# Value and gate columns of the recurrence as a seven-product Strassen stage per segment, x prepared elsewhere, the recurrence one lag deeper

## The chip, the cores and the metric

The kernel runs on one core of one Trainium2 chip. The metric is the device time of one execution in microseconds (us); before the change it is 2083.62 us, the median of three runs (2082.52 to 2084.76).

## The reference, cut to what matters

One decoder layer on x of 2048 tokens by 1024 features. Everything is float32.

```python
h = rms_norm(x, norm_w) * (1 + scale) + shift          # scale, shift, gate from c @ w_ada
proj = h @ w_in                                        # 1024 -> 6656 columns
aq, ak, av, ag, rq, rf, ri, rg = split(proj)           # 1024, 256, 256, 1024, 4 x 1024
attn = sliding_window_attention(rope(norm(aq)), rope(norm(ak)), av, sinks) * silu(ag)
f = lb + (1 - lb) * sigmoid(rf)
rec = hgrn2_chunkwise(rq, f, ri)                       # 8 heads, chunks of 64 tokens
rec = rms_norm(rec, rec_norm_w) * silu(rg)
out = x + gate * (concat(attn, rec) @ w_out)
```

The change concerns the columns ri (the value) and rg (the gate) of the projection: 2 x 1024 of the 6656 columns.

## The kernel before, in words

Each large product is made in split precision: an operand is rounded to a high part (ScalarE, `split_hi`, `round_x`) and the rest is subtracted (VectorE, `split_lo`, `rest_x`), and TensorE makes three products, high x high, high x low and low x high (`split_products`, L498 to L503). Every matmul of the projections and of the output is issued from L502.

The tokens are worked in two segments of 1024. A segment has two phases, and at the end of each all five queues (SP, TensorE, ScalarE, VectorE, GpSimd) meet (`arrive`, `meet`).

- Ahead of the first segment, w_ada is loaded in six parts of 2 MB, TensorE multiplies it by c, and VectorE reads out shift, scale and gate (L484 to L496, L1007 to L1069).
- Attention: four groups of four heads, eight token blocks of 128 each (`att_iter`). In group 0 of a segment the blocks of x are prepared between the iterations: square, root on GpSimd, scaling, eight transposes on TensorE (`transpose_x`, L551), modulation, rounding, rest. Three stages of the attention of earlier blocks (scores, probabilities, output) run beside the projections of the present block.
- Recurrence: eight heads, two quads of 512 tokens each (`rec_iter`, L647 to L703). For a quad TensorE makes f and q (columns by tokens: 24 matmuls of 512 columns each), then value and gate as rows (`project_nat`, L542: two halves of 48 matmuls of 256 columns), and beside them the chunk products of the quad before it: k_inv x q_dec and the transposes of k_out (L664, L667), the chunk states (L678), the two parts of the output (L694, L700). ScalarE makes tanh, the logarithm and three exponentials, VectorE the running sum, the states (L1274) and the normed rows (L1287), GpSimd three products and a root.
- The output: 16 rows of blocks, each 96 matmuls of 512 columns (`out_rows`, L742).

The order of the work on each engine is the order in which its queue is written; there is no planner. SP issues all transfers in one queue. Spills of the attention and of the recurrence go to DRAM and come back for the output (`load_mixed`).

Of the kernel before, what the change touches and what calls it, by code (L numbers as in the profile page):

```python
# [16 lines left out]
KT = D // P  # L17
SEQ = 2048
# [14 lines left out]
UNITS = GROUPS + RHEADS  # L33
# [4 lines left out]
MOD_T = 3 * D // HALF  # L38
WO_PARTS = 8
WO_F = FT // WO_PARTS  # L40
WO_EARLY = 5
# [7 lines left out]
ATT_UNIT, REC_UNIT = REG[0] + REG[1], KT * 4 * RK  # L49
LAG = 3  # L50
TWO_PI = 2.0 * np.pi
# [5 lines left out]


def hybrid_layer(nc, x, cT, pos, norm_w, w_ada, b_cols, b_gate, w_in, qk_w, sinks, rec_w, lbT, w_out,
                 ident_d, masks_d, causal_d, freq_d, out, mixed_T, mixed):  # L60
    with ExitStack() as ctx:
# [4 lines left out]


        def sbuf(where, name, shape, dt=F32):
            return where.enter_context(nc.sbuf_tensor(name, shape, dt))

        ident = sbuf(ctx, "ident", [P, P])
        gate_bc = sbuf(ctx, "gate_bc", [P, D])

        unsplit = ExitStack()
        h_f = sbuf(unsplit, "h_f", [P, KT, SEG])
        x_early = sbuf(unsplit, "x_early", [P, KT, SEG])

        ang, turns, cosv, sinv = [x_early[:, :, (NBLK - 3) * P + q * (HD // 2):(NBLK - 3) * P + (q + 1) * (HD // 2)]
                                  for q in range(4)]

        wa = [h_f[:, t * KT // 2:(t + 1) * KT // 2, :].rearrange("p k (a n) -> p (k a) n", n=HALF) for t in range(2)]
        wa += [sbuf(unsplit, f"wa{t}", [P, KT, HALF])[:] for t in (2, 3)]
        unsplit.close()
        main = ExitStack()
        h_lo = sbuf(main, "h_lo", [P, KT, SEG], F32R)
        h_hi = sbuf(main, "h_hi", [P, KT, SEG], F32R)
        w_hi = [sbuf(main, f"w_hi{r}", [P, REG[r]], F32R) for r in range(2)]
        w_lo = [sbuf(main, f"w_lo{r}", [P, REG[r]], F32R) for r in range(2)]
        raw = [sbuf(main, f"raw{r}", [P, REG[r]]) for r in range(2)]


        rot = sbuf(main, "rot", [P, NBLK, 2, 2, HD])
        masks = sbuf(main, "masks", [P, SEGS, 2 * P])
        mask_first = sbuf(main, "mask_first", [P, 2 * P])
        k_carry = sbuf(main, "k_carry", [P, GROUPS, 2, P])
        v_carry = sbuf(main, "v_carry", [P, GROUPS, HD])
        mod_a = sbuf(main, "mod_a", [P, KT])
        x_ss = sbuf(main, "x_ss", [P, 2])
        x_var = sbuf(main, "x_var", [P, 2])
        x_rinv = sbuf(main, "x_rinv", [P, 2])  # L100
        mod_b = sbuf(main, "mod_b", [P, KT])
        head_par = sbuf(main, "head_par", [P, RHEADS, 4])
        sink_bc = sbuf(main, "sink_bc", [P, HEADS])
        sink_neg = sbuf(main, "sink_neg", [P, HEADS])
        qk_wt = sbuf(main, "qk_wt", [P, 2, HD])
        rec_wt = sbuf(main, "rec_wt", [P, RK])
        minus_half = sbuf(main, "minus_half", [P, 8])
        half_pi = sbuf(main, "half_pi", [P, 1])
        freq = sbuf(main, "freq", [P, HD // 2])
        pos_f = sbuf(main, "pos_f", [P, SEQ // P])  # L110
        causal = sbuf(main, "causal", [P, P], I32)
        state = sbuf(main, "state", [P, RHEADS, RK])

        pre = ExitStack()
        wa += [sbuf(pre, f"wa{t}", [P, KT, HALF])[:] for t in (4, 5)]
        wa_sum = [sbuf(pre, f"wa_sum{i}", [P, HALF]) for i in range(2)]
        c_in = sbuf(pre, "c_in", [P, KT])
        c_th = sbuf(pre, "c_th", [P, KT])
        c_act = sbuf(pre, "c_act", [P, KT])
        c_bc = sbuf(pre, "c_bc", [P, KT, P])  # L120
        ones = sbuf(pre, "ones", [P, P])
        diag_junk = sbuf(pre, "diag_junk", [P, 4, P])
        mod_cols = sbuf(pre, "mod_cols", [P, 2 * KT])
        b_col = sbuf(pre, "b_col", [P, 2 * KT])
        b_gate_s = sbuf(pre, "b_gate_s", [P, D])
        norm_s = sbuf(pre, "norm_s", [P, KT])
        pos_i = sbuf(pre, "pos_i", [P, SEQ // P], I32)
        lb_in = sbuf(pre, "lb_in", [P, 2, RHEADS])
        lb_t = sbuf(pre, "lb_t", [P, 4, RHEADS])
        pre.close()  # L130

        att = ExitStack()
        xb = [sbuf(att, f"xb{i}", [P, D]) for i in range(2)]
        sq = sbuf(att, "sq", [P, GH + 1, HD])
        q_ss = sbuf(att, "q_ss", [P, GH + 1])
        q_var = sbuf(att, "q_var", [P, GH + 1])
# [1426 lines left out]
```

## Time and profile before

| | us |
|---|---|
| Median of three runs | 2083.62 |
| The profiled execution, its own time | 2087.02 |
| Its span from the first to the last instruction | 2085.2 |
| TensorE busy | 1983.0 (95%) |
| VectorE, ScalarE, GpSimd busy | 920.2, 850.3, 565.0 |
| Mean granted TensorE clock | 0.980 of full speed |

The span is what the views of the trace are measured in. A row of the page's groups gives the line, the engine, the operation, the tiles written and read, the shape, the count, the busy time and the mean time of one. The chain of waits is followed back from the last instruction; a piece has its start, its length and what ran in it.

### The profile page before, as it was taken

Reading aid. Unit: us, or ns where it says so; the run is one execution under the profiler, and the core shown is the slowest. Engines: PE = TensorE matmul, PEld = TensorE weight load, DVE = VectorE, ACT = ScalarE, POOL = GpSimd, SP = SyncE. Lnnn points to the kernel's source line nnn. Section 1 sums busy time; section 2 is a strip of 40 time slices with the busy share of each in tenths; the row PEclk is TensorE's granted clock in tenths of the full one; section 3 lists DMA queues with packets and bytes.
Section 4 is the critical chain, followed back from the end, with each engine's and each line's share of the span. In section 5 each row is a group of like instructions: output and inputs, shape, how many; then the busy total and the mean of one; then the engine's idle time right before and its main releaser. Section 6 shows DMA issues by size and latency. Waiting matters only on the chain.

```text
span 2085.2 us, 36824 instructions
## 1 busy us (share of the span) xinstructions
PE 1983.0 (95%) x13180; PEld 1742.7 (84%) x13180; DVE 920.2 (44%) x2492; ACT 850.3 (41%) x2141; POOL 565.0 (27%) x889
## 2 busy tenths in 40 slices
PE   6789999989999999778999998999999989999999
PEld 2778898879999998678889887999998878888887
DVE  6665546534434444366564553434444444222221
ACT  1565555643333434356555654333434332101000
POOL 1444545421222222244554441222222210000000
PEclk9899999999999999889999999999999989999999
DMA  9201011011111111320101011111011135222221
GB/s 353 85 21 64 11 63 48 17 49 52 51 50 37 31 41 46 107 82 24 62 14 63 28 37 49 52 51 37 31 41 47 50 142 196 81 101 91 91 80 41
DMA packets 81264, 136.32 MB, mean 65 GB/s; under 512 B 5025, under 2 KB 58785, under 8 KB 75041
## 3 DMA queue, kind: packets, MB, share of 16 engines
q1 hardware_dynamic: 81184, 135.34, 18.5%
q8 instruction: 41, 0.67, 0.1%
q14 instruction: 39, 0.31, 0.1%
HBM read 110.16 MB, written 25.17 MB: 65 GB/s over the span
## 4 chain that ended last, share of the span: by engine, by line
PE 85%; issue 4%; ACT 3%; DVE 3%; POOL 2%; SPq 1%; DMA 0%; POOLq 0%; DVEq 0%; ACTq 0%
PE bank L502 68%; PE bank L643 3%; PE bank L603 2%; PE bank L630 2%; PE bank L678 2%; PE bank L700 2%; PE bank L694 1%; PE bank L664 1%; ACT sm L828 1%; POOL q_rinv L1390 1%; DVE h_f L1090 1%; DVE sm L1130 1%; PE bank L738 1%; PE bank L667 1%; SPq L347 1%
## 5 line engine op out<-in xcount | busy, mean ns | idle before, releaser
L502 PE MATMUL bank<-w_hi,h_hi 128*128 128x256 f32 (+1 forms) x1536 | 476.8, 310 | 10.4 <-DVE w_lo L1077 8.7
L502 PE MATMUL bank<-w_lo,h_hi 128*128 128x256 f32 (+1 forms) x1536 | 465.0, 303 | 0.0
L502 PE MATMUL bank<-w_hi,h_lo 128*128 128x256 f32 (+1 forms) x1536 | 464.6, 302 | 0.0
L502 PE MATMUL bank<-h_hi,w_hi 128*128 128x256 f32 (+1 forms) x1024 | 356.8, 348 | 0.4 <-DVE qn L1197 0.4
L502 PE MATMUL bank<-h_hi,w_lo 128*128 128x256 f32 (+1 forms) x1024 | 346.2, 338 | 0.0
L502 PE MATMUL bank<-h_lo,w_hi 128*128 128x256 f32 (+1 forms) x1024 | 345.7, 338 | 0.0
L502 PEld LDWEIGHTS bank<-w_hi,h_hi 128*128 128x128 f32 x1536 | 295.3, 192 | 23.1 <-issue 9.7
L502 PEld LDWEIGHTS bank<-w_lo,h_hi 128*128 128x128 f32 x1536 | 295.6, 192 | 0.0
L502 PEld LDWEIGHTS bank<-w_hi,h_lo 128*128 128x128 f32 x1536 | 295.3, 192 | 0.0
L502 PEld LDWEIGHTS bank<-h_hi,w_hi 128*128 128x128 f32 x1024 | 196.0, 191 | 39.1 <-issue 20.9
L502 PEld LDWEIGHTS bank<-h_lo,w_hi 128*128 128x128 f32 x1024 | 195.7, 191 | 21.2
L502 PEld LDWEIGHTS bank<-h_hi,w_lo 128*128 128x128 f32 x1024 | 196.1, 192 | 18.2
L502 PE MATMUL bank<-wo_hi,m_hi 128*128 128x512 f32 x512 | 203.0, 397 | 5.6 <-DVE m_lo L1326 5.6
L502 PE MATMUL bank<-wo_hi,m_lo 128*128 128x512 f32 x512 | 200.2, 391 | 0.0
L502 PE MATMUL bank<-wo_lo,m_hi 128*128 128x512 f32 x512 | 200.0, 391 | 0.0
L828 ACT ACTIVATE sm<-sm,neg_m 128x256 f32<-128x256 f32 x256 | 127.1, 498 | 155.5 <-DVE sink_d L1140 155.5
L1077 DVE TENSOR_TENSOR w_lo<-raw,w_hi 128x1024 fp32r<-128x1024 f32 (+1 forms) x96 | 126.0, 1354 | 13.0 <-ACT w_hi L796 12.9
L928 ACT ACTIVATE o_sq<-bank 128x128 f32<-128x128 f32 x128 | 33.7, 278 | 231.5 <-PE bank L700 231.5
L859 ACT ACTIVATE sm<-sm,r_den 128x256 f32<-128x256 f32 x256 | 109.4, 504 | 36.2 <-DVE r_den L1164 36.1
L1287 DVE SCALAR_TENSOR_TENSOR r_mix<-bank,o_rinv,rg_w 128x128 f32<-128x128 f32 x128 | 36.0, 344 | 191.0 <-POOL o_rinv L1390 191.0
L502 PEld LDWEIGHTS bank<-wo_hi,m_hi 128*128 128x128 f32 x512 | 96.5, 189 | 25.1 <-issue 5.9
L1450 POOL TENSOR_TENSOR b_rest<-b_cum 128x512 f32<-128x512 f32 x32 | 33.3, 1042 | 300.0 <-DVE b_cum L1258 300.0
(180 smaller groups left out, 3184.5 us busy)
## 6 DMA issues: line engine op xcount, KB each, us to landing
raw<-in_w_in SPq DMA_DIRECT2D x40, 1024.0 KB, 6.9
raw<-in_w_in SPq DMA_DIRECT2D x8, 1536.0 KB, 6.2
wa<-in_w_ada SPq DMA_DIRECT2D x8, 1024.0 KB, 13.2
mixed_cols<-o_mix SPq DMA_DIRECT2D x64, 128.0 KB, 1.8
mixed_rows<-r_mix SPq DMA_DIRECT2D x32, 256.0 KB, 2.3
m_cols<-mixed_cols SPq DMA_DIRECT2D x16, 512.0 KB, 4.1
m_rows<-mixed_rows SPq DMA_DIRECT2D x16, 512.0 KB, 4.8
wo_raw<-in_w_out SPq DMA_DIRECT2D x8, 1024.0 KB, 10.7
```

The costliest lines, as they stand in the source:

```text
L502: mm = pe.matmul(dst, a, b, start=(first and m == 0), stop=(last and m == 2))
L603: mm = pe.matmul(bank[7][e * HD:(e + 1) * HD, 0:2 * P], vv[:, j + half, :], pT[j % 2][:, e:GH:2, half, :], start=(half == 0), stop=(half = ...
L630: mm = pe.matmul(bank[2 + h % 2][:, (h // 2) * 2 * P:(h // 2 + 1) * 2 * P], tq[j % 2][lo:lo + HD, h // 2, :], tk[lo:lo + HD, j:j + 2, :], ...
L643: mm = pe.transpose(bank[5 + h // 2][:, at:at + P], sm[j % 2][:, h, half * P:(half + 1) * P], ident[:])
L678: mm = pe.matmul(bank[6 - c % 2][:, b * P:(b + 1) * P], k_nat[lo:lo + CH, b * P:(b + 1) * P], r_v[lo:lo + CH, b, :], start=True, stop=True)
L700: mm = pe.matmul(bank[7][c * CH:(c + 1) * CH, b * P:(b + 1) * P], q_dec[jt][:, t0:t0 + CH], s_in[jt][:, 2 * b + c, :], start=False, stop=T ...
L828: act.activation(sm[j % 2][:, h, :], sm[j % 2][:, h, :], ACT.Exp, bias=neg_m[j % 2][:, h:h + 1], accum_out=den[j % 2][:, h:h + 1]).then_in ...
L859: a = act.activation(sm[j % 2][:, h, :], sm[j % 2][:, h, :], ACT.Identity, scale=r_den[j % 2][:, h:h + 1])
L928: act.activation(o_sq[:, b, :], bank[7][:, b * P:(b + 1) * P], ACT.Square, accum_out=o_ss[:, b:b + 1]).then_inc(oss_ok, 1)
L1077: dve.tensor_tensor(w_lo[r][:, half], raw[r][:, half], w_hi[r][:, half].bitcast(F32), ALU.subtract).then_inc(lo_ok[r], 1)
L1287: dve.scalar_tensor_tensor(r_mix[jt][:, b, :], bank[7][:, b * P:(b + 1) * P], o_rinv[:, b:b + 1], rg_w[:, b, :], ALU.mult, ALU.mult).then_ ...
L1450: pool.tensor_tensor(b_rest[:].rearrange("p (c t) -> p c t", t=CH), b3[:, :, CH - 1:CH].to_broadcast([P, NCH, CH]), b3, ALU.subtract).then ...
```

## The change

The projection of ri and rg leaves the recurrence. Ahead of the attention of each segment stands a new stage (`gemm_unit`): the product of 1024 tokens x 1024 features with 2 x 1024 columns is cut into two units of 1024 columns, and each unit is done as a 2 x 2 block product with seven block products instead of eight (Strassen's scheme in Winograd's form). A block product is 512 tokens x 512 features x 512 columns, 48 matmuls of 512 columns (four token blocks, four feature blocks, three split products). The sums of blocks that the scheme wants are made on VectorE (S1, S2, the weights' t2) and on GpSimd (t1, t3, t4 of the weights, s4 of the tokens), each 128 x 2048 elements; each operand is then split by ScalarE and VectorE. The results are combined on VectorE, the gate columns get their SiLU, GpSimd multiplies them by the norm's weight, and both are spilled to DRAM (`nat`). The recurrence loads them back (`nat_load`).

x of segment 0 is loaded first of all, ahead of w_ada, scaled and transposed while w_ada arrives (`square_first`, `normalize_first`, `copy_first`). x of segment 1 is scaled and transposed in half blocks, one in each of the 16 steps of the recurrence of segment 0 (`square_half`, `root_half`, `transpose_half`, `copy_half`), spilled, and loaded back when the last projection of that recurrence is done. The adaLN gate (the last third of w_ada) is computed in the recurrence of segment 1 (`gate_piece`, `gate_row`). The output's weights are all loaded after the last projection, and the first mixed rows after the last spill. The keys and values carried between segments go through DRAM.

The recurrence is written out step by step: f of step t, outputs of step t-2, chunk products of t-1, q of t, chunk states of t-1. Its weights come in one piece for f and q, two heads ahead.

The core of the diff:

```diff
-            def project_nat(w, j, half, fresh):
-
-                for b in range(2):
-                    mm = project(1, w, fresh and half == 0 and b == 0,
-                                 lambda k: project_rows(bank[2 + half][:, b * 2 * RK:(b + 1) * 2 * RK], 1,
-                                                        j * QB + half * 2 + b, 0, 2 * RK, 2 * RK, k))
...
+                for c in range(4):
+                    bank_free(c)
+                    for k in range(KH):
+                        ah, al = operand(c, k)
+                        wh, wl = g_hi[N % 2][:, k, :], g_lo[N % 2][:, k, :]
+                        mm = split_products(ring(n, at + c)[:, :], ((ah, wh), (ah, wl), (al, wh)), fresh and k == 0,
+                                            k == KH - 1, skip_group_check=not fresh)
+                    mm.then_inc(blk_ok, 1)
...
+                strassen(n, s, 0, 0, True, in_h(0, 0), free_p1)
+                strassen(n, s, 1, 0, False, in_h(KH, 0), lambda c: pe.wait_ge(p1_ok, 4 * n + c + 1))
+                strassen(n, s, 2, 4, True, in_s(S2), free_p6)
+                strassen(n, s, 3, 8, True, in_h(0, QUAD), free_p7)
+                strassen(n, s, 4, 12, True, in_s(S1), free_p5)
+                strassen(n, s, 5, 12, False, in_s(S4), lambda c: pe.wait_ge(comb_ok, comb(n, COMB_22, c)))
+                strassen(n, s, 6, 16, True, in_h(KH, QUAD), free_p4)
```

VectorE's and GpSimd's part at the start of a segment's first unit (`gemm_sums`, `weights_t2` on VectorE, `gemm_unit` on GpSimd):

```diff
+                dve.tensor_tensor(s_f[S1][:], h_f[:, K1, T2], h_f[:, K2, T2], ALU.add).then_inc(sums_ok, 1)
...
+                dve.tensor_tensor(s_f[S2][:], s_f[S1][:], h_hi[:, K1, T1].bitcast(F32), ALU.subtract).then_inc(sums_ok, 1)
...
+                dve.tensor_tensor(s_f[S2][:], s_f[S2][:], h_lo[:, K1, T1].bitcast(F32), ALU.subtract).then_inc(sums_ok, 1)
+                weights_t2(n)
...
+                dve.tensor_tensor(h_f[:, K1, T2], h_hi[:, K1, T1].bitcast(F32), h_f[:, K1, T2], ALU.subtract
+                                  ).then_inc(sums_ok, 1)
...
+                dve.wait_ge(s4_raw, 2 * s + 1)
+                lo(s_lo[S2][:], s_f[S2][:], s_hi[S2][:], o0 + 3)
...
+                pool.tensor_tensor(g_raw[B11][:], g_raw[B12][:], g_raw[B11][:], ALU.subtract).then_inc(t1_ok, 1)
...
+                pool.tensor_tensor(g_raw[B12][:], g_raw[B22][:], g_raw[B12][:], ALU.subtract).then_inc(t3_ok, 1)
...
+                    pool.tensor_tensor(s_f[S4][:], h_hi[:, K2, T1].bitcast(F32), s_f[S2][:], ALU.subtract).then_inc(s4_raw, 1)
```

TensorE's new order in the recurrence, and what SP does after its last projection:

```diff
+                    if 1 <= t < REC_T:
+                        pe.wait_ge(fth_ok, T)
+                        project_f(s, h, j)
+                    if t >= 2:
+                        outputs(T - 2, t - 2)
+                    if 2 <= t <= REC_T:
+                        chunk_products(T - 1, t - 1)
+                    if s + 1 < SEGS and t < 2 * NBLK:
+                        transpose_half(t)
...
+                    if 1 <= t < REC_T:
+                        pe.wait_ge(qdec_ok, T)
+                        project_q(s, h, j)
...
+                    if 1 <= t <= REC_T:
+                        chunk_states(s, T - 1, t - 1)
...
+                            sp.wait_ge(ga_done, 2)
+                            load_out_weights(range(WO_PARTS))
...
+                if s == SEGS - 1:
+                    load_mixed(0, 0)
```

## Rows read from the trace of the kernel before

**Rows 1.** The page: busy time by engine, and the shares of the chain.

```profile
PE 1983.0 (95%) x13180; PEld 1742.7 (84%) x13180; DVE 920.2 (44%) x2492; ACT 850.3 (41%) x2141; POOL 565.0 (27%) x889
...
PE 85%; issue 4%; ACT 3%; DVE 3%; POOL 2%; SPq 1%; DMA 0%; POOLq 0%; DVEq 0%; ACTq 0%
```

**Rows 2.** Stages: start:end, length, busy per engine, PE clock, DMA share, GB/s.

```profile
0.00:53.00 53.00, 33.14 (x76) 14.54 (x76) 32.77 (x92) 9.85 (x16) 8.29 (x15) 0.92 0.98 348
...
163.00:416.00 253.00, 249.63 (x1871) 224.04 (x1870) 135.49 (x499) 147.82 (x466) 119.86 (x233) 1.00 0.12 42
...
442.50:864.00 421.50, 421.49 (x3040) 382.13 (x3041) 169.23 (x382) 160.35 (x335) 94.51 (x93) 0.99 0.15 50
...
889.50:1252.30 362.80, 342.66 (x2521) 309.67 (x2521) 205.27 (x693) 215.20 (x644) 169.38 (x327) 0.98 0.13 44
```

**Rows 3.** The chain of waits (start, length, what): recurrence, segment 0; an output row.

```profile
462.57 0.44 PE bank L667 x4
...
469.58 5.93 PE bank L502 x48
...
477.44 11.42 PE bank L502 x72
504.61 11.42 PE bank L502 x72
...
1733.10 16.37 PE bank L502 x72
```

**Rows 4.** Groups by shape: operation, tiles, shape, count, busy us, mean ns.

```profile
L1077 DVE TENSOR_TENSOR w_lo<-raw,w_hi 128x1024 fp32r<-128x1024 f32 x76 | 90.6, 1234 | 12.9 <-ACT w_hi L796 12.9
...
L1418 POOL TENSOR_TENSOR rc<-qn,rot 128x256 f32<-128x256 f32 x64 | 47.1, 736 | 53.9 <-DVE qn L1197 53.9
...
L1456 POOL TENSOR_TENSOR k_inv<-k_f,e_nb 128x512 f32<-128x512 f32 x32 | 41.1, 1283 | 25.5 <-ACT e_nb L920 22.4 <-issue 3.1
...
L1426 POOL TENSOR_TENSOR rs<-qn,rot 128x32 f32<-128x32 f32 x128 | 39.8, 332 | 0.0
```

**Rows 5.** Instructions of VectorE and GpSimd in order of time, two stretches.

```profile
159.01 2.42 DVE L1077 TENSOR_TENSOR w_lo<-raw,w_hi 128x1024 fp32r<-128x1024 f32 x2 [0.89 <-ACT w_hi L796]
...
159.08 2.46 POOL L1426 TENSOR_TENSOR rs<-qn,rot 128x32 f32<-128x32 f32 x2
...
885.68 0.72 POOL L1482 TENSOR_TENSOR x_early<-x_early 128x256 f32<-128x256 f32 x1
...
885.81 1.67 DVE L1097 TENSOR_TENSOR h_lo<-h_f,h_hi 128x1024 fp32r<-128x1024 f32 x1 [1.18 <-ACT h_hi L815]
...
886.56 1.63 POOL L1480 TENSOR_SCALAR x_early<-x_early 128x256 f32<-128x256 f32 x1 [0.16 <-POOL x_early L1482]
...
887.41 4.14 DVE L1077 TENSOR_TENSOR w_lo<-raw,w_hi 128x1536 fp32r<-128x1536 f32 x2
```

**Rows 6.** The chain of waits, attention to recurrence in segment 0.

```profile
415.92 5.75 PE bank L502 x24
...
440.18 1.97 PE bank L603 x8
```

**Rows 7.** Transfers: issues, KB each, median us to landing.

```profile
mixed_cols<-o_mix SPq DMA_DIRECT2D x64, 128.0 KB, 1.8
...
xb<-in_x SPq DMA_DIRECT2D x12, 512.0 KB, 3.7
```

**Rows 8.** The chain of waits, segment 0 to segment 1.

```profile
857.86 5.96 PE bank L502 x48
...
875.70 0.52 DVE r_mix L1287 x2
...
889.27 2.27 DVE w_lo L1077
```

**Rows 9.** The chain of waits, last recurrence to output.

```profile
1694.32 5.96 PE bank L502 x48
...
1716.71 10.05 PE bank L502 x36
```

More of the change, by code:

```diff
@@ L81, in hybrid_layer @@
[L81 to L88, printed above, removed]
@@ new lines, in row @@
+        def row(at, *tensors):
+            made = []
+            for name, shape, dt in tensors:
+                made.append(place(at, name, shape, dt))
+                at += 4 * int(np.prod(shape[1:]))
+            return made, at
+        h_lo = place(0, "h_lo", [P, KT, SEG], F32R)
+        h_hi = place(KT * SEG * 4, "h_hi", [P, KT, SEG], F32R)
+        h_f = place(0, "h_f", [P, KT, SEG])
+        x_first = [place(KT * SEG * 4 + m * D * 4, f"x_first{m}", [P, KT, P]) for m in range(NBLK)]
@@ L377, in att_spill, with gemm, attention @@
+            def gemm(s):
+                for u in range(GU):
+                    gemm_unit(s, u)
+                done = (s + 1) * GU
+                sp.wait_ge(nat_u2, 64 * done)
+                sp.wait_ge(nat_u3, 128 * done)
+                for c in range(3):
+                    sp.wait_ge(nat_c[c], 16 * done * (2 if c == 0 else 1))
+            def attention(s):
                 def att_spill(g, i):
@@ L705, in _, with gate_row, transpose_half @@
-            with pe.Fori(0, SEGS) as s:
-                meet(pe, seg_phase(s, 0))
-                transpose_x(s, 0)
-                transpose_x(s, 1)
+            def gate_row(t):
+                pe.wait_ge(ga_ok, KT * (t + 1))
+                geq(pe, ga_done, t)
+                pe.matmul(bank[6][:, :], g_ones[:], ga_sum[:], start=True, stop=True).then_inc(ga_mm, 1)
+            def transpose_half(t):
+                m, half = t // 2, t % 2
+                pe.wait_ge(x_nrm, NBLK + m + 1)
+                pe.wait_ge(x_ev_v, NBLK + t)
+                for k in range(KH):
+                    mm = pe.transpose(bank[6][:, k * P:(k + 1) * P], xb[m % 2][:, half * KH + k, :], ident[:])
+                mm.then_inc(x_T, 1)
@@ new lines, in chunk_states @@
+            def chunk_states(s, T, t):
+                b = t % 2
+                pe.wait_ge(knat_ok, T + 1)
+                pe.wait_ge(rv_in[b], 16 * (s * (REC_T // 2) + t // 2 + 1))
+                geq(pe, st_ok, NCH * T)
+                for c in range(NCH):
+                    lo, q = CH * (c % 2), c // 2
+                    mm = pe.matmul(bank[2 + c % 2][:, tokens(q)], k_nat[lo:lo + CH, tokens(q)], r_v[b][lo:lo + CH, q, :],
+                                   start=True, stop=True)
+                mm.then_inc(u_ok, 1)
@@ L709, in _ @@
+            for s in range(SEGS):
+                for u in range(GU):
+                    gemm_unit(s, u)
+                pe.wait_ge(comb_ok, 20 * GU * (s + 1))
+                arrive(pe)
                 for i in range(NBLK):
@@ L716, in _ @@
                 arrive(pe)
[L718 to L727 removed]
+                recurrence(s)
                 arrive(pe)
@@ L852, in att_iter @@
                     split_hi(0, w + 1)
-                if head and first and i + 2 < NBLK:
-                    modulate_x(s, i + 2)
                 if two:
@@ L950, in _ @@
+            gemm_start(0)
+            for s in range(SEGS):
+                for u in range(GU):
+                    gemm_unit(s, u)
+                rotary_angles(s)
+                arrive(act)
+                meet(act, att_phase(s))
                 for i in range(NBLK):
@@ L1486, in _ @@
+            for s in range(SEGS):
+                for u in range(GU):
+                    gemm_unit(s, u)
+                arrive(pool)
+                meet(pool, att_phase(s))
                 for i in range(NBLK):
```

1770 lines of the change are left out of this document (1051 added, 719 removed).

## The prediction

> **What bounds the kernel now.** I read the busy times first: TensorE is busy for 1983.0 us of the span and makes 85% of the chain; no other engine reaches half [rows 1]. So each matmul removed counts in full, as long as nothing else becomes late. The stages come next [rows 2]: groups 1 to 3 of the attention take 253.0 us, 84.3 each, with TensorE busy for 249.6, while the four groups of segment 1 take 362.8, so group 0, between whose iterations x is prepared, takes 109.8. Last the chain in the recurrence [rows 3]: two like pieces start 27.17 us apart, a quad; TensorE never pauses. All sums are made against the profiled execution (time 2087.0, span 2085.2), 3.4 us above the median of 2083.6; I take the 3.4 off at the end. A measurement of this kernel tells about 0.2% (4 us) from no change.
>
> **The matmuls.** Removed: 96 matmuls of 256 columns a quad, 48 in 5.93 us [rows 3], so 11.86 us, times 32 quads: 379.5 us. Added: 28 block products of 48 matmuls of 512 columns. The nearest row is the output's, with the same operand forms: 72 in 16.37 us [rows 3], 227.4 ns each, 10.9 us a product, 305.6 us in all. Net -73.9. A quad of the recurrence falls from 27.17 to 15.3 us.
>
> **x out of group 0.** Group 0 should cost what the others do, 84.3. To that I add 6 for the hand-over: TensorE has block 0 projected (7 us), but ScalarE and VectorE first finish the last gate tile, the sine tables and the last spill, 8 to 9 us after the last product. 90.3 for 109.8: -19.5 a segment, -39. x of segment 1 comes back as 16 groups of four transposes at 0.44 [rows 3]: +7.
>
> **The start.** 0 to 53 us ran at 348 GB/s [rows 2]. The first product needs x of segment 0 (4.2 MB) and four parts of w_ada (8.4 MB): 12.6 MB, 36 us, landed at about 38. Then the product with w_ada and its readout, which I put at 7, and modulating, rounding, rest, and the first weights' rest, four steps of about 2.3 [rows 4]: first product at 54.5, against a first projection at 53.2: +1.3, 4 either way. The half clock at a start is new beside the product: 36 output matmuls took 10.05 instead of 8.2 [rows 9], so +2 a segment, +4.
>
> **The new stage's other engines.** This is where the answer lies. Ahead of product 2 of a segment's first unit VectorE must do, after it has released product 0, one modulation and ten subtractions or additions of 128x2048: h_lo, weights' rest, S1, S2 twice, t2, two for a21, rest of S2, weights' rest. Two of 128x1024 take 2.42 in a row [rows 5], so each is 2.3 to 2.4 (1234 ns for half of one [rows 4]): 25 us with the modulation. Products 0 and 1 last 21.8+2 = 24. Alone, VectorE would be 1 us late. But GpSimd runs t1, t3 and s4 (two passes) in that stretch, and t2 waits for t1, the rest of S2 for s4. A GpSimd operation costs 736 ns at 256 elements and 1283 at 512 [rows 4], 547 for each 256 more: 4.6 us at 2048.
>
> Do the two engines run side by side? Rows 5 say no. Two GpSimd products of 32 elements, 332 ns each otherwise [rows 4], took 2.46 us, the same stretch as VectorE's two subtractions of 2.42. In the other direction, VectorE's h_lo started 0.13 us behind a GpSimd operation and took 1.67 instead of 1.23, and its two subtractions of 1536 took 4.14 where 2 x 1.8 is due. Each waits for the other's whole operation. The Trainium skill says this too (SBUF — State Buffer, "Who interferes with whom"): a VectorE instruction with two SBUF inputs takes the read port that GpSimd reads through, for the whole instruction. The trace agrees, with the 2.46 us above. By that rule the 44 us below stand in the sum, and if it did not hold here, 1 us a segment would.
>
> So VectorE's 25 us get t1, t3 and two passes of s4 put between them: 25 + 4 x 4.6 = 43.4; TensorE stands still for 43.4 - 24 = 19.4, and 1.3 is lost to the clock after it. I take 20.7. The ends: 1 (no exclusion), and 20.7 + 4.6 = 25.3 if one pass of t4 also slips in. In the second unit t1 starts only when GpSimd has multiplied the last gate rows, and t2 of that unit is late by 1 to 3: 1.2. Sum: +22 a segment, +44. The other products have 3 to 10 us in hand: their combinations (four of 0.6), one or two splits (2.3 each) and four SiLU tiles (0.4) fit in 10.9.
>
> **The recurrence.** In 421.5 us, 15.5 quads, VectorE is busy for 169.2, ScalarE for 160.4, GpSimd for 94.5 [rows 2]: 10.9, 10.3 and 6.1 a quad. VectorE loses the gate (0.8) and half of the weights' rest (1.2) and gains a half block of x (1.1) or, in four steps of segment 1, a piece of the gate's sum (3); so 10 to 13 in a step of 15.3. The loop from f to the k products is some 15 us, but one lag deeper it is wanted only 7 us into the next step. I cost it at nothing; if that cover is gone, each us is paid 32 times. The start costs: before, value and gate filled TensorE while the queues met; now it waits. The last attention output ends at 442.15 [rows 6], the last spill lands 1.8 after its issue [rows 7], the meeting is 3.2 after the end. In segment 0, SP then issues x (3.7 to land [rows 7]) and ScalarE squares it ahead of its first tanh: TensorE stands still for 11 and is slow after it; in segment 1 gate loads and a VectorE sum stand ahead of q. Against 421.7 before from that end to the last projection, less 189.8 for value and gate, I get 10 and 8 more: +18, ends 8 (meeting alone, 2 x 4) and 28.
>
> **The ends of the segments.** Before, the last projection ended at 863.8 and rows were done at 876.2, 12.4 later; the first projection of segment 1 came at 889.6 once weights' rest (to 891.5 for its second half) allowed it [rows 8]: 25.8. Now two steps follow the last projection: states and output of quad 14, then of quad 15 (each 3 of states, 2 of output, 1.2 of squares, 1.4 of root, 1.3 of rows, partly behind each other): 21.5. Then four VectorE steps of 2.3: 31. +5.2. x (4.2 MB at 348 GB/s) lands after 14 and is covered. At the output: before, 1700.3 to 1716.7 [rows 9], 16.4. Now all 8.4 MB of weights stand ahead of the first mixed rows in the queue, 24 us, the rows 3 and their split 3 more: about 31. +14.6.
>
> **Sum.** -73.9 - 39 + 7 + 1.3 + 4 + 44 + 18 + 5.2 + 14.6 = -18.8. 2087.0 - 18.8 - 3.4 = 2064.8; I say 2065. The bounds of the unknown terms (port 20.7 to 25.3 here, starts 8 to 28, hand-over and ends 6 each way) give 2052 to 2081 for this case.
>
> **Rivals.** (1) The port is free: VectorE and GpSimd overlap in operations this long. Then 44 shrinks to about 2: 2023. For it: no row has a GpSimd operation above 1.3 us against VectorE, and it may give way inside. Against: all of rows 5. (2) Slower: nothing of VectorE and GpSimd overlaps in the stage, combinations from PSUM included, and it ends on the two queues instead of TensorE. In a segment's stage VectorE has 29 operations of 2.3 in SBUF, a modulation and the attention's weights, 75 us, and 36 of combinations and SiLU; GpSimd has ten of 4.6, 32 gate rows of 0.7 and the angles, 76: 187, and the chains leave gaps of at least 8: 195 against 177 in my sum, +36: 2101. It decides from 9 us more a segment. Against: GpSimd and VectorE's states from PSUM overlap in the recurrence today. (3) The recurrence's step is not TensorE's: a wait of 0.5 us a step, at VectorE's turn between q and the states, where it has little in hand: +16, 2081, no change. (4) The stage does what it says; less work is not in doubt.
>
> **Chances.** The forecast's case 0.60 (nearly all faster, its top end no change), rival 1 0.17, rival 2 0.12, rival 3 0.11 (about a third of it faster, a third the same, a third slower). Faster by over 0.2%: 0.56 + 0.17 + 0.03 = 0.76; same 0.04 + 0.04 = 0.08; slower 0.12 + 0.04 = 0.16. The range goes from rival 1 to just above no change: 2020 to 2088, leaving out rival 2 and the tails, 0.18. The likeliest case's own range is 2052 to 2081.
>
> **What would show it.** Right: block products in pieces of 10.9 us in the chain, TensorE idle by about 19 us ahead of the third product of each segment and there alone, ended by the weights' rest; VectorE's operations of 128x2048 at 2.3 alone and at up to 7 where GpSimd's run; steps of 15.3 (15.7 in segment 0); the output 31 after the last projection. Wrong: no pause at the third product (rival 1), pauses before most products (rival 2), or waits in every step of the recurrence (rival 3).

## The result, and the profile after the change

The change makes the kernel slower: 2099.32 us, median of five runs (2092.75 to 2100.98), against 2083.86 for the kernel before in the same session; the ratio is 1.0069, 95% interval 1.0052 to 1.0085. Run again as a control it gave 2096.28 and 1.0054 (1.0040 to 1.0067). The forecast was 2065 with a range of 2020 to 2088. The profiled execution took 2097.52, its span is 2095.7.

Busy time by engine and shares of the chain, from the page of the changed kernel, to set beside [rows 1]:

```profile
PE 1922.5 (92%) x11436; PEld 1629.3 (78%) x11436; DVE 1106.1 (53%) x2494; ACT 876.7 (42%) x2073; POOL 704.5 (34%) x949
...
PE 48%; DVE 5%; issue 3%; ACT 1%; POOL 1%; DMA 1%; SPq 0%; POOLq 0%; DVEq 0%; ACTq 0%
```

TensorE has 60.5 us less busy time, and the span is 10.5 longer: it stands still for 173 us where it stood for 102. What it waits for, longest first (engine, tile and line that waits, the one waited for, us in total, times, longest):

```profile
PE bank L683 <- DVE g_lo L1386: 75.6, 7, 25.5
PE bank L967 <- DMA m_rows<-mixed_rows: 14.5, 1, 14.5
PE bank L875 <- DVE xb L1617: 12.1, 1, 12.1
```

g_lo is the weights' rest in the new stage: 49.5 of the 75.6 us stand ahead of the third products, 23.2 ahead of the first products of the two stages. The stages by windows (the columns of [rows 2]): the two new stages, a recurrence, the attention of segment 1, the output:

```profile
54.00:239.00 185.00, 158.72 (x672) 129.65 (x672) 138.73 (x100) 57.84 (x67) 92.93 (x46) 0.91 0.23 77
...
581.00:878.00 297.00, 271.43 (x1720) 225.24 (x1719) 161.30 (x394) 148.18 (x326) 87.52 (x110) 0.95 0.35 107
878.00:1075.00 197.00, 158.34 (x672) 129.65 (x672) 147.86 (x113) 68.48 (x82) 99.55 (x48) 0.89 0.29 101
1078.00:1417.00 339.00, 333.98 (x2471) 302.00 (x2472) 175.96 (x629) 192.81 (x597) 163.54 (x315) 0.99 0.14 48
...
1740.00:2096.00 356.00, 351.80 (x1607) 290.81 (x1605) 81.23 (x113) 33.50 (x45) 0.00 (x0) 1.00 0.24 83
```

In the first stage VectorE is busy for 139 of 185 us and GpSimd for 93; neither is full, and the records of both hold waits for each other. Nearly all of the loss stands in one place of each stage. TensorE's instructions in order of time, those behind a pause, in the first stage:

```profile
103.93 0.80 PE L683 MATMUL bank<-g_hi,s_hi 128*128 128x512 f32 x1 [23.95 <-DVE g_lo L1386]
104.53 0.63 PE L683 MATMUL bank<-g_lo,s_hi 128*128 128x512 f32 x1
...
110.07 0.44 PE L683 MATMUL bank<-g_hi,s_lo 128*128 128x512 f32 x1
110.35 0.40 PE L683 MATMUL bank<-g_hi,s_hi 128*128 128x512 f32 x1
```

A product of 48 starts at 54.04, the second at 68.81 (1.28 us late), and then TensorE stands for 23.95 us ahead of the third. After it 14 matmuls start 0.43 us apart instead of 0.23, at the lower of the two clock levels. In the second stage the same pause is 25.51, ahead of 940.20. What holds it up are VectorE and GpSimd, in order of time:

```profile
53.90 10.45 DVE L1401 TENSOR_SCALAR h_f<-h_f,mod_a,mod_b 128x512 f32<-128x512 f32 x4
54.13 4.73 POOL L1827 TENSOR_TENSOR g_raw<-g_raw 128x2048 f32<-128x2048 f32 x1 [33.55 <-DVE g_lo L1386]
59.01 4.61 POOL L1830 TENSOR_TENSOR g_raw<-g_raw 128x2048 f32<-128x2048 f32 x1
64.28 2.28 DVE L1397 TENSOR_TENSOR h_lo<-h_f,h_hi 128x2048 fp32r<-128x2048 f32 x1
...
75.53 2.28 DVE L1393 TENSOR_TENSOR g_t<-g_raw 128x2048 f32<-128x2048 f32 x1
75.69 6.54 POOL L1833 TENSOR_TENSOR s_f<-h_hi,s_f 128x2048 f32<-128x2048 f32 x1 [12.07 <-DVE s_f L1433]
77.73 6.65 DVE L1436 TENSOR_TENSOR h_f<-h_hi,h_f 128x2048 f32<-128x2048 f32 x1
```

Alone, VectorE's operation takes 2.28 and GpSimd's 4.6. From 77.7 on each record holds the wait for the other's: four of VectorE's in a row start 6.4 to 6.7 us apart (77.73, 84.42, 90.80, 97.30). The weights' rest ends at 103.9, 49.9 us after the first product. In the second stage t1 starts later, because its weights land later, and t1 and t3 meet the two passes of S2 (6.58 and 6.57) instead of the modulation; there too six of VectorE's operations are lengthened, by 4.3 each.

### The profile page after: what moved, and what is told of

It is laid out like the page before. It is cut to its first block, busy times and chain, and to the rows that moved or that the text cites. A ratio compares the mean times of both kernels' runs of the same rounds, so it can differ in the third digit from the quotient of the medians.

```text
span 2095.7 us, 32145 instructions
## 1 busy us (share of the span) xinstructions
PE 1922.5 (92%) x11436; PEld 1629.3 (78%) x11436; DVE 1106.1 (53%) x2494; ACT 876.7 (42%) x2073; POOL 704.5 (34%) x949
## 3 DMA queue, kind: packets, MB, share of 16 engines
q1 hardware_dynamic: 144928, 182.80, 25.7%
## 4 chain that ended last, share of the span: by engine, by line
PE 48%; DVE 5%; issue 3%; ACT 1%; POOL 1%; DMA 1%; SPq 0%; POOLq 0%; DVEq 0%; ACTq 0%
PE bank L683 39%; PE bank L859 2%; PE bank L827 1%; PE bank L846 1%; PE bank L891 1%; PE bank L904 1%; DVE g_lo L1386 1%; PE bank L917 1%; PE bank L967 1%; PE bank L884 1%; DVE w_lo L1455 0%; DVE s_in L1662 0%; DMA m_rows<-mixed_rows 0%; DVE g_t L1393 0%; PE bank L906 0%
## 5 line engine op out<-in xcount | busy, mean ns | idle before, releaser
L683 PE MATMUL bank<-w_hi,h_hi 128*128 128x384 f32 x512 | 178.6, 349 | 8.3 <-DVE u L1516 6.4
L683 PE MATMUL bank<-w_hi,h_lo 128*128 128x384 f32 x512 | 173.2, 338 | 0.0
L683 PE MATMUL bank<-w_lo,h_hi 128*128 128x384 f32 x512 | 172.7, 337 | 0.0
L1916 POOL TENSOR_TENSOR k_out<-b_cum 128x512 f32<-128x512 f32 x32 | 34.3, 1073 | 351.3 <-DVE b_cum L1697 351.3
L1568 DVE SCALAR_TENSOR_TENSOR o_mix<-bank,g_s 128x128 f32<-128x128 f32 x128 | 31.2, 286 | 180.8 <-PE bank L827 180.8
L683 PE MATMUL bank<-g_hi,s_hi 128*128 128x512 f32 x192 | 77.7, 404 | 51.1 <-DVE g_lo L1386 51.1
L683 PE MATMUL bank<-g_hi,h_hi 128*128 128x512 f32 x256 | 101.9, 398 | 24.4 <-DVE g_lo L1386 24.4
L1809 POOL TENSOR_SCALAR q_var<-q_ss 128x5 f32<-128x5 f32 x64 | 12.7, 198 | 303.4 <-issue 292.2
L683 PEld LDWEIGHTS bank<-wo_hi,m_lo 128*128 128x128 f32 x512 | 96.7, 189 | 20.7
L683 PEld LDWEIGHTS bank<-wo_lo,m_hi 128*128 128x128 f32 x512 | 96.8, 189 | 19.3
## 6 DMA issues: line engine op xcount, KB each, us to landing
wa<-in_w_ada SPq DMA_DIRECT2D x8, 1024.0 KB, 12.1
```

The lines of the kernel that those rows point to most:

```text
L683: mm = pe.matmul(dst, a, b, start=(first and m == 0), stop=(last and m == 2), **more)
L1568: a = dve.scalar_tensor_tensor(o_mix[j % 2][:, t, :], bank[7][:, t * P:(t + 1) * P], 0.5, gate[t], ALU.mult, ALU.mult)
L1916: pool.tensor_tensor(k_out[b][:].rearrange("p (c t) -> p c t", t=CH), b3[:, :, CH - 1:CH].to_broadcast([P, NCH, CH]), b3, ALU.subtract).th ...
```

## The experiments

Theory P (port): VectorE and GpSimd take turns in this stretch, an operation at a time; the pause is the sum of both, and GpSimd's part of it is there only because of when its operations are issued. Rivals: A, VectorE's own chain sets the pause; B, what is taken out of the stretch is paid later. The table has what the runs gave. "To product 3" is from the start of a segment's first block product to that of the third, "stage" to the end of the last, both for the segments 0 and 1, read from TensorE's instructions in order of time.

| run | us | ratio to before | to product 3 | pause | stage |
|---|---|---|---|---|---|
| changed kernel | 2099.3 | 1.0069 | 49.9, 49.9 | 24.0, 25.5 | 184.8, 184.8 |
| the same, control | 2096.3 | 1.0054 | 49.9, 49.9 | 23.9, 25.3 | 183.6, 183.4 |
| t4 late | 2076.6 | 0.9961 | 41.3, 41.3 | 15.4, 17.5 | 174.7, 174.7 |
| four late | 2075.7 | 0.9955 | 32.9, 33.5 | 8.1, 9.2 | 173.3, 174.0 |
| t4 as a fill | 2076.9 | 0.9959 | 41.3, 41.3 | 15.3, 16.9 | 174.1, 174.3 |
| t1, s4 on VectorE | 2067.8 | 0.9916 | 28.8, 28.8 | 4.1, 4.6 | 169.5, 169.4 |
| all together | 2054.0 | 0.9853 | 28.8, 29.0 | 5.0, 4.2 | 169.4, 169.6 |
| spread | 2043.7 | 0.9802 | 28.8, 28.9 | 5.1, 4.2 | 163.9, 164.0 |
| ScalarE modulates | 2042.9 | 0.9794 | 28.6, 28.7 | 4.6, 4.1 | 163.5, 163.7 |

**t4 of the weights later.**

```diff
-                pool.wait_ge(wlo_ok, N0 + 2)
+                pool.wait_ge(wlo_ok, N0 + 3)
                 pool.tensor_tensor(g_raw[B21][:], g_raw[B21][:], g_raw[B22][:], ALU.subtract).then_inc(t4_ok, 1)
```

> One edit: GpSimd's t4 (two passes of 128x2048) waits until the third product's weights have their rest. Port theory (VectorE and GpSimd take turns, an operation at a time): in the changed kernel the rest of S2 and the weights' rest take 6.58 each beside t4, and 2.28 without it; the pause ahead of product 3 of each stage falls from 24.0 and 25.5 us by 2 x 4.3 = 8.6 to about 15.5 and 17, and the whole by 17 us to about 2082. Rival A (VectorE's chain sets the pause by itself and the long records are only waiting that costs nothing): pause and time as before the edit, 2099. Rival B (the turns are only moved): the pause shrinks but comes back ahead of product 4 or 5 of the stage, 2095 to 2099.

Measured: 2076.63 (2075.86 to 2079.76), 0.9961 (0.9947 to 0.9975). One number of a wait turns the change from a loss into a small gain. The two VectorE operations that stood beside t4, and t4 itself:

```profile
84.36 6.46 DVE L1439 TENSOR_TENSOR h_f<-h_f,h_lo 128x2048 f32<-128x2048 f32 x1
90.75 2.28 DVE L1397 TENSOR_TENSOR s_lo<-s_f,s_hi 128x2048 fp32r<-128x2048 f32 x1
92.95 2.28 DVE L1386 TENSOR_TENSOR g_lo<-g_t,g_hi 128x2048 fp32r<-128x2048 f32 x1
95.29 0.80 PE L683 MATMUL bank<-g_hi,s_hi 128*128 128x512 f32 x1 [15.36 <-DVE g_lo L1386]
95.31 4.60 POOL L1837 TENSOR_TENSOR g_raw<-g_raw 128x2048 f32<-128x2048 f32 x1 [6.63 <-DVE g_lo L1386]
```

The third product comes 8.6 us earlier in either stage, as P says. The stages are 10.0 shorter each than in the first profiled execution of the changed kernel and 8.8 and 8.6 shorter than in the control's, so what goes beyond the 8.6 is within what the changed kernel differs by from one execution to the next (14 slow matmuls behind each pause in the first, 8 and 7 in the control, 8 and 7 here). The median falls by 22.7 us, by 19.7 against the control, for the 17 expected. A falls, and of B there is little here: 0.6 and 0.7 ahead of product 4.

**Four of GpSimd's six operations later.**

```diff
                 pool.tensor_tensor(g_raw[B11][:], g_raw[B12][:], g_raw[B11][:], ALU.subtract).then_inc(t1_ok, 1)
+                if u == 0:
+                    pool.wait_ge(sums_ok, 5 * s + 3)
+                    pool.tensor_tensor(s_f[S4][:], h_hi[:, K2, T1].bitcast(F32), s_f[S2][:], ALU.subtract).then_inc(s4_raw, 1)
+                    pool.wait_ge(wlo_ok, N0 + 3)
...
                 pool.tensor_tensor(g_raw[B12][:], g_raw[B22][:], g_raw[B12][:], ALU.subtract).then_inc(t3_ok, 1)
```

(the second pass of s4 and t4 follow t3)

> One edit: in a segment's first unit only t1 and the first pass of s4 stay in the stretch; t3, the second pass of s4 and t4 wait for the third product's weights' rest. Port theory: four GpSimd operations of 4.3 to 4.6 leave the pause ahead of product 3: 24.0 and 25.5 become about 7 and 8, the whole falls by 35 us to about 2064; t3 is then wanted for product 4 and may cost 0 to 5 us there, so 2064 to 2074. Rival A: nothing changes, 2099. Rival B (moved turns are paid again): pauses of 5 to 10 ahead of products 4, 6 and 7, 2085 or more.

Measured: 2075.73 (2071.44 to 2077.83), 0.9955 (0.9941 to 0.9969). The third product comes 17.0 and 16.4 us earlier, as P says, but the stage is only 1.4 and 0.8 shorter than with t4 alone late, and the time only 0.9: the range of P (2064 to 2074) was missed. In segment 0 TensorE now waits ahead of later products:

```profile
86.50 0.80 PE L683 MATMUL bank<-g_hi,s_hi 128*128 128x512 f32 x1 [8.09 <-DVE g_lo L1386]
99.93 0.50 PE L683 MATMUL bank<-g_hi,h_hi 128*128 128x512 f32 x1 [0.53 <-DVE g_lo L1386]
113.18 0.50 PE L683 MATMUL bank<-g_hi,s_hi 128*128 128x512 f32 x1 [2.07 <-DVE g_lo L1386]
```

With three smaller ones behind these (0.8, 0.6, 0.8) and 9 slow matmuls after the one of 2.07, about 7 of the 8.4 us come back. VectorE's operations there are of 6.7, beside GpSimd's of 6.7. So B holds in part: where GpSimd's operations stand back to back, turns are paid again when they hold up a weights' rest that the next product wants. Turns are not all of it. VectorE also waits 5.99 us for the spill of the first gate columns, which GpSimd's gate rows, now behind t4, release:

```profile
119.11 2.48 DVE L1486 TENSOR_TENSOR u<-bank,u 128x512 f32<-128x512 f32 x4 [5.99 <-DMA nat_rows<-u]
```

**t4 as a fill of zeros.** Left out: t4, so the seventh product has zero weights.

```diff
-                pool.tensor_tensor(g_raw[B21][:], g_raw[B21][:], g_raw[B22][:], ALU.subtract).then_inc(t4_ok, 1)
+                pool.memset(g_raw[B21][:], 0.0).then_inc(t4_ok, 1)
```

(both passes, at their old place)

> t4's two passes are replaced by fills of the same tile with zeros: GpSimd writes but reads nothing (left out: t4, so product 7 has zero weights). If the turns come from reading SBUF, the rest of S2 and the weights' rest go back to 2.3 each and the pause falls by 8.6 to about 15.5, the time to about 2082, as with t4 late. If any GpSimd access takes the turn, both stay at 2.3 plus the fill's own time (a fill alone is not in the trace, 2 to 4.6 us): pause 20 to 25, time 2090 to 2099.

Measured: 2076.9 (2073.14 to 2078.72), 0.9959 (0.9941 to 0.9973).

```profile
88.27 1.80 POOL L1837 MEMSET g_raw<- 128x2048 f32 x1
90.12 1.80 POOL L1839 MEMSET g_raw<- 128x2048 f32 x1
90.39 2.28 DVE L1397 TENSOR_TENSOR s_lo<-s_f,s_hi 128x2048 fp32r<-128x2048 f32 x1
92.60 2.28 DVE L1386 TENSOR_TENSOR g_lo<-g_t,g_hi 128x2048 fp32r<-128x2048 f32 x1
```

The second fill runs from 90.12 to 91.92, VectorE's subtraction from 90.39 to 92.67, and neither is lengthened. So what these two take turns at is GpSimd's reading, not its writing. The Trainium skill says so (SBUF — State Buffer, "Who interferes with whom"): two SBUF inputs on VectorE collide with a GpSimd instruction that reads SBUF, not with one that only writes. The trace agrees.

**t1 and the first pass of s4 on VectorE**, on top of the four late (GpSimd's own two are taken out).

```diff
+                dve.tensor_tensor(g_raw[B11][:], g_raw[B12][:], g_raw[B11][:], ALU.subtract).then_inc(t1_ok, 1)
                 weights_t2(n)
+                dve.tensor_tensor(s_f[S4][:], h_hi[:, K2, T1].bitcast(F32), s_f[S2][:], ALU.subtract).then_inc(s4_raw, 1)
```

> On top of the run with four GpSimd operations late: t1 and the first pass of s4 of a segment's first unit are done on VectorE, so that GpSimd has nothing in the stretch. A 128x2048 operation costs 2.28 us on VectorE and takes 4.3 to 4.6 of VectorE's time on GpSimd. Port theory: the pauses of 8.1 and 9.2 us ahead of product 3 fall by 2 x 2.2 = 4.4 each, to about 4 and 5, the whole from 2075.7 to about 2067. Rival (VectorE's own work is the bound, and GpSimd's last two operations hide in it): VectorE gets 4.6 us more, pauses 12 to 14, 2084.

Measured: 2067.79 (2064.65 to 2069.55), 0.9916 (0.9899 to 0.9932), pauses 4.1 and 4.6: P to within 1 us. VectorE got two operations more and the product came 4.1 and 4.7 earlier. From the changed kernel to here the third product comes 21.1 us earlier: six GpSimd operations out, two of 2.29 in, so each of the six had cost (21.1 + 4.6) / 6 = 4.3.

**The mixed rows ahead of the output weights.**

```diff
                             sp.wait_ge(ga_done, 2)
+                            sp.wait_ge(rec_out[0], (SEGS * (REC_T // 2) - 1) * 16)
+                            load_mixed(0, 0)
                             load_out_weights(range(WO_PARTS))
...
-                if s == SEGS - 1:
-                    load_mixed(0, 0)
-                else:
+                if s < SEGS - 1:
```

> One edit on SP: the first block of mixed rows is loaded ahead of the eight parts of the output weights, not behind them. If the 14.5 us in which TensorE waits for the mixed rows are the queue's, they go; then the chain is r_mix of the last quad at 1713.3, the meeting, the rounding of the rows 1.1 to 2.3 and their rest 3: first output product about 9 us earlier (1717 to 1718 instead of 1726.7), the whole about 2090. Rival: the weights' own arrival and rounding pace the first output rows, one part of two a microsecond or more, and the end moves by only 0 to 4 us: 2095 to 2099.

Measured: 2085.50 (2081.63 to 2090.17), 1.0001 (0.9991 to 1.0011). TensorE's first output product stood behind 14.50 for the mixed rows and 0.76 for their rest; now:

```profile
1718.72 0.77 PE L683 MATMUL bank<-wo_hi,m_hi 128*128 128x512 f32 x1 [5.59 <-DVE m_lo L1748]
```

From the last output of the recurrence to this product it is 7.7 us, in the changed kernel 17.2 (1709.5 to 1726.70): 9.5. But that last output itself ends 1.6 us later (1711.1), so from the end of the last projection, at 1693.4 in both, the first output product comes 25.3 instead of 33.3 us later: 8.0 won. The two profiled executions, 2097.52 and 2090.17, are 7.4 apart, which this explains. The rest of the 11 to 14 us between the medians I can't place; it is inside the scatter of the changed kernel (8 us in one set of runs).

**The first half block of x one step later**, in the recurrence of segment 0 (square, root and scaling at the end of step 0, both transposes in step 1; TensorE's part of the edit):

```diff
-                    if s + 1 < SEGS and t < 2 * NBLK:
+                    if s + 1 < SEGS and 1 <= t < 2 * NBLK:
+                        if t == 1:
+                            transpose_half(0)
                         transpose_half(t)
```

> On the changed kernel alone: in the recurrence of segment 0 the first half block of x is squared, normalised and transposed in step 1 instead of at the very start, ahead of everything. Theory X (as predicted: the load and the squares of x make TensorE's 12.1 us at the start of this recurrence): they go, with some 2 of slow clock after them, and the time falls by 8 to 12 us to 2088 to 2091. Theory L (the loop from f over the root of the gate to q_dec and the k products is as long by itself, as in segment 1, where no x stands ahead and the start costs as much or more): TensorE waits as long for k_f and q_dec instead, and the time stays at 2096 to 2101.

Measured: 2090.10 (2088.62 to 2093.66), 1.0027 (1.0016 to 1.0039), within theory X's range. But by the trace the wait is not gone: 12.14 us have become 5.31 for k_f, 0.55 and 1.27 for x. From the end of the attention's last product to the next stage it is 278.5 instead of 283.3, so 4.8 of the 6 to 9 between the medians are this. So the load and the squares of x cost 5 us, less than theory X had. What is left is not theory L's loop over f either: ScalarE's k_f itself stands behind the meeting of the queues, which waits for the attention's last spills.

```profile
610.92 0.60 ACT L1224 ACTIVATE k_f<-bank 128x512 f32<-128x512 f32 x1 [6.83 <-SPq L321]
```

It is the same in segment 1, where no x stands ahead: 6.22 us of ScalarE's idling end with the meeting, and TensorE waits 4.70 for k_f. No wait for q_dec follows in this run.

**All together:**

> All edits together: GpSimd out of the stretch ahead of product 3, t1 and the first pass of s4 on VectorE, mixed rows ahead of the output weights, the first half block of x one step later. If they add up: 2099.3 - 23.6 (four late) - 9 (on VectorE) - 13.8 (rows first) - 0 to 12 (x later) = 2041 to 2053. If the half clock after a pause takes a part back or the pauses only move, 2055 to 2065. Either way under the kernel before (2085).

Measured: 2053.98 (2052.35 to 2054.75), 0.9853 (0.9837 to 0.9870), 1 us above the range of the sum.

**GpSimd's late operations spread**, on top of it: t3, the four gate rows, the second pass of s4 after the fourth product's weights, t4 after the fifth's.

```diff
                 if u == 0:
+                    for c in range(4):
+                        gate_rows(q0 + c, u3[c])
+                    pool.wait_ge(wlo_ok, N0 + 4)
                     pool.wait_ge(s4_raw, 2 * s + 1)
...
-                pool.wait_ge(wlo_ok, N0 + 2)
+                pool.wait_ge(wlo_ok, N0 + (5 if u == 0 else 2))
...
-                for c in range(4):
-                    gate_rows(q0 + c, u3[c])
+                if u > 0:
+                    for c in range(4):
+                        gate_rows(q0 + c, u3[c])
```

> On top of all edits together: GpSimd's late operations are spread. t3 stays behind the third product's weights, then come the four first gate rows, the second pass of s4 behind the fourth product's weights and t4 behind the fifth's. In the run before, pauses of 2.0, 1.0, 1.1 and 0.6 us stand ahead of products 5 to 7 of the first unit, in which each operation of VectorE of 128x2048 takes 6.7 beside one of GpSimd. Port theory: the turns no longer fall into the chain of the next weights; some 3 us of pauses and 2 of slow clock go per segment: 2044 to 2050. Rival (the sum of both engines' work in the first unit is the bound, wherever it stands): the same pauses later, 2052 to 2055.

Measured: 2043.66 (2040.41 to 2045.20), 0.9802 (0.9789 to 0.9814), at the lower end of P's range: the stages are 5.5 shorter each. The same operations of both engines are done; only where they meet has changed:

```profile
90.39 2.83 DVE L1388 TENSOR_TENSOR g_lo<-g_raw,g_hi 128x2048 fp32r<-128x2048 f32 x1
95.17 4.61 POOL L1850 TENSOR_TENSOR s_f<-s_f,h_lo 128x2048 f32<-128x2048 f32 x1
98.14 3.79 DVE L1399 TENSOR_TENSOR s_lo<-s_f,s_hi 128x2048 fp32r<-128x2048 f32 x1
101.86 2.28 DVE L1388 TENSOR_TENSOR g_lo<-g_raw,g_hi 128x2048 fp32r<-128x2048 f32 x1
104.21 4.61 POOL L1852 TENSOR_TENSOR g_raw<-g_raw 128x2048 f32<-128x2048 f32 x1 [4.43 <-DVE g_lo L1388]
```

The two weights' rests took 6.71 and 6.68 in the run of all together; here 2.83 and 2.28. The rival, that the sum of both engines' work is the bound, falls. How much of the 5.5 is turns is not shown: the gate rows now stand ahead of t4, and VectorE's wait of 6.1 us in each stage for the spill of the gate columns, with TensorE's pauses of 1.00 and 1.15 in the first stage behind it, is gone too.

**What the clock takes after a pause.** On the changed kernel alone:

```diff
+                if u == 0:
+                    free_p6(0)
+                    for i in range(100):
+                        pe.matmul(ring(n, 4)[:, :], h_hi[:, KH + i % KH, 0:P], h_hi[:, KH + i % KH, 0:QUAD],
+                                  start=True, stop=True)
                 strassen(n, s, 2, 4, True, in_s(S2), free_p6)
```

> On the changed kernel alone: in the pause ahead of product 3 of each segment TensorE does 100 matmuls of 512 columns on data that lies ready, into a bank that product 3 overwrites (22.8 us of 24.0 and 25.5); no work of the kernel moves. What the pause costs beside its own length: in the changed kernel the first 14 matmuls of product 3 run at half clock, 0.45 us each instead of 0.23. If the clock falls because TensorE stands still, they run at full clock, and the time falls by 2 x 3 = 6 us to 2093; if the filler makes product 3 late, by at most 1 us a segment back. Rival (the clock falls for another reason): 2099 or above.

Measured: 2090.49 (2085.63 to 2091.77), 1.0027 (1.0016 to 1.0037). In segment 0 it did what was expected: one slow matmul, where the changed kernel has 14 in one execution and 8 in the control; stage 182.3 instead of 184.8 (control 183.6). The stretch from 79.8 us, with the filler and without it (columns of [rows 2]; the clock is the column 1.00 and 0.66):

```profile
79.80:120.00 40.20, 38.53 (x171) 31.57 (x169) 36.70 (x16) 12.99 (x14) 25.57 (x8) 1.00 0.16 53
```

```profile
79.80:120.00 40.20, 16.25 (x59) 13.08 (x59) 33.99 (x15) 10.60 (x14) 24.60 (x8) 0.66 0.15 53
```

In segment 1 the filler left 3.20 us idle, 14 matmuls were slow again, and the stage took 185.1 (control 183.4). Against the first profiled execution the two stages together are 2 us shorter, against the control's not at all. So in segment 0 the full clock was kept with the filler in the pause, in segment 1 it was not, and no gain in time is shown; where the 6 to 9 us between the medians are from stays open.

**ScalarE does the last modulation**, on top of the spread version, and the **control** (no edit):

```diff
+                for k in range(KH, KT):
+                    a = act.activation(h_f[:, k, T2], h_f[:, k, T2], ACT.Identity, bias=mod_b[:, k:k + 1],
+                                       scale=mod_a[:, k:k + 1])
+                a.then_inc(hmod_v, 1)
...
-                modulate(K2, T2, s, 2)
```

> On top of the spread version: the last modulation (four of 128x512, second half of k and of tokens) is done by ScalarE, not VectorE, in the stretch ahead of product 3. If VectorE's queue of operations is what is left of the pause there (5.1 and 4.2 us), it falls by the 2.1 us of the four to 3.0 and 2.1: 2037 to 2041. If a wait for ScalarE (rounding) takes its place, 2042 to 2046.

> The changed kernel as it is, run again beside the kernel before, to bound what a single edit must move to be told from the scatter (its five runs went from 2092.8 to 2101.0): 2095 to 2101, pauses of 24.0 and 25.5 us ahead of product 3 in the same places.

Measured, ScalarE's modulation: 2042.85 (2038.92 to 2045.86), 0.9794 (0.9778 to 0.9811), the rival's range, and no change from the spread version that the scatter would show. By the trace the third product came 0.2 us earlier, not 2.1. VectorE got the 2.1 us and spent 1.5 of them waiting for ScalarE, whose rounding of the weights now stands behind the modulation:

```profile
55.50 1.89 ACT L1053 ACTIVATE g_hi<-g_raw 128x2048 fp32r<-128x2048 f32 x1
57.42 2.29 DVE L1392 TENSOR_TENSOR g_lo<-g_raw,g_hi 128x2048 fp32r<-128x2048 f32 x1 [1.53 <-ACT g_hi L1053]
```

The control came out as expected, 2096.28 (2091.77 to 2097.21), with pauses of 23.9 and 25.3. It bounds all of the above: two sets of the same kernel differ by 3 us in the median, and two profiled executions of it by 5.7 us of span and 1.2 to 1.4 us in a stage.

## Why the prediction was wrong, point by point

It named the mechanism and the place and got the sign wrong. Two steps failed. The turns of VectorE and GpSimd ahead of product 3 were counted as four operations of 4.6 us, 18.4; six of 4.3, 25.7, stand there. And the removed matmuls were priced from one piece of the chain, with what is left of the step taken to cost the same as before, so a quad was to fall by 11.86; it fell by 11.48. The sum was small (-18.8), and all of its large misses had one sign. The terms against the profiled run, in us, misses as added time:

| step | predicted | measured | miss |
|---|---|---|---|
| matmuls removed, 32 quads | -379.5 | 32 x 11.48 = -367.4 | +12.1 |
| pauses ahead of product 3 | 2 x 19.4 | 23.95 + 25.51 | +10.7 |
| slow clock after them | 2 x 1.3 | 3.1 + 3.0 | +3.5 |
| products 1 and 2 | 2 x 24 | 25.9 + 24.4 | +2.3 |
| recurrence starts | 10 + 8 | 8.3 + 12.0 | +2.3 |
| last projection to output | 31 | 33.3 | +2.3 |
| all others together (what remains) | | | -3.9 |

The misses make 29.3, the difference of the spans (2095.7 against 2085.2 - 18.8); with the 3.4 taken off at the end of the forecast and the 1.8 from this execution to the median it is the 34.5 from 2064.8 to 2099.3. The table is of one execution. The control's has a span of 2090.0 and 8 and 7 slow matmuls behind its pauses for 14 and 14, so the smaller rows, the slow clock among them, are not firm; the first two are, as the steps and the pauses repeat.

**The removed matmuls** were priced at 11.86 a quad, twice the 5.93 of one piece of the chain. By the starts of the matmuls, 48 narrow ones took 5.85 both times in the kernel before, and the 24 wide ones behind them 5.47:

```profile
469.51 0.39 PE L502 MATMUL bank<-w_hi,h_hi 128*128 128x256 f32 x1
...
475.36 1.05 PE L694 MATMUL bank<-r_v,a_T 128*128 128x128 f32 x8
...
477.37 0.39 PE L502 MATMUL bank<-w_hi,h_hi 128*128 128x256 f32 x1
...
483.22 0.40 PE L502 MATMUL bank<-h_hi,w_hi 128*128 128x512 f32 x1
...
488.69 1.05 PE L664 MATMUL bank<-q_dec,k_inv 128*128 128x128 f32 x8
489.58 0.60 PE L667 MATMUL bank<-ident,k_out 128*128 128x128 f32 x4
```

So the piece's price was 0.08 too high, twice. The other part is in what stays: without the narrow matmuls ahead of them the same 24 wide ones take 5.58 (1489.66 to 1495.24), and k_inv x q_dec, which stood behind wide matmuls and took 0.89, takes 1.00 (1497.24 to 1498.24). 11.86 less 2 x 0.08 and 2 x 0.11 is 11.48. The step of a quad in the chain after, where a piece goes from end to end (1.09 for that product):

```profile
1489.73 5.67 PE bank L683 x24
1495.40 0.89 PE bank L884 x8
1496.29 1.02 PE bank L891 x16
1497.31 1.09 PE bank L904 x8
1498.40 0.44 PE bank L906 x4
1498.84 5.49 PE bank L683 x24
1504.33 1.09 PE bank L917 x16
```

Its sum is 15.69, against 27.17: 11.48 a quad. The prediction expected 15.3. The 0.4 is near the 0.5 of rival 3, but it is not that rival: nothing waits in these steps. The added products were right: the last 240 matmuls of the first stage took 54.69, 228 ns each for 227.4.

**The pause** is the step that decided the sign; its mechanism was right and its size wrong. "t1, t3 and two passes of s4 put between them": it was six operations, not four. VectorE's own part was right: with GpSimd out of the stretch it is 28.8 us with two operations more, so 24.2 for the 25 of the prediction. t4 is released by the second product's weights' rest (done at 68.8 us), so it stands in GpSimd's queue behind s4 and starts with the next turn. The prediction had one pass of t4 as its upper end, 25.3 with the clock; the pauses with it came to 27.1 and 28.5. That these two passes alone are enough to turn the sign is shown: with t4 late the kernel is at 0.9961. That they cost 4.3 each rather than 4.6 is shown too.

**Rival 1** (the port is free) is out: four of VectorE's operations took 6.5 each. **Rival 2** gave 2101, 2 us from the result, but by another cause. It wanted nothing of the two engines to overlap in the whole stage, and pauses before most products; there was a long pause ahead of one only; from the third product to the ninth the stage ran at 11.3 a product, slow matmuls included, and at 10.9 from the tenth on, and it took 184.8 for the rival's 195. Its price was a coincidence.

**The other steps.** First product 54.04 (54.5). x out of group 0: from the end of the stage to the recurrence's first f 342.3 and 342.5 (343.3). Steps with half blocks of x 16.12, 0.43 more than without. Second stage 30.0 after the last projection (31). Recurrence starts: segment 0 cheaper (8.3 for 10), segment 1, where no x stands ahead, dearer (12.0 for 8). There TensorE waits 4.70 for k_f, behind the meeting, then 2.73 for q_dec and 2.79 for the states, each behind a piece of the gate's sum on VectorE (3.7 and 5.6 us), which the prediction had named and priced too low. Output start 33.3 (31): the mixed rows landed behind the weights, 30.5 us after the last projection for the 27 of the prediction; with the rows ahead of the weights only 8.0 of the 33.3 went, as the last outputs of the recurrence come late by themselves.

**The range** of the forecast's case, 2052 to 2081, took in t4 with one pass only and gave the price of the removed matmuls, the largest number of the sum, no width at all. Its own bounds, added up (9.2 for one pass of t4 in each segment, 10 for the starts, 6 for the ends), would reach 2090.

## What to carry to other kernels

In a difference of two large numbers, price the whole period of the steady state that stays, not only the piece that goes, and give that price a width: here the piece's price was 0.16 too high in a quad and the pieces that stayed got 0.22 dearer, 12 us in 32 quads. Where VectorE and GpSimd both read SBUF in long operations, add their times, as the runs here bear out; then ask of each GpSimd operation when it is released and when it is wanted, because its place in the queue, not its amount, made a difference of 24 us here and, with the gate rows moved ahead, of 10 more when the late ones were spread. This algorithm with fewer multiplications moved its cost to the sums, and these fell due at the start of the stage, before TensorE had work to hide them.

## What the hardware showed that was not expected

- A fill by GpSimd (1.80 us) and a subtraction by VectorE ran side by side, unlengthened.
- VectorE's modulation has one SBUF input beside its per-partition scalars, and took turns all the same: four of 128x512 in 10.45 us beside t1 and t3, in 1.92 without them.
- After the filler TensorE kept the full clock over 1.67 us of idling in segment 0, and lost it for 14 matmuls after 3.20 us in segment 1. After like pauses of 24 to 25.5 us the unchanged kernel lost it for 14 matmuls in one execution and for 8 and 7 in another.
- The same narrow chunk products took 0.89 or 1.09 us of the chain by what ran ahead of them.
